# A two-block transformer kernel: x split for the second block without its inverse norm, three additions of eight on GpSimd, and weights, loads and chunks in another order

## The chip, the cores and the metric

The kernel runs on one core of a Trainium2 chip. The metric is the device time of one execution in microseconds, the median of several. All arithmetic is in fp32. The projections work with both operands split in two parts: a rounded high part and the rest, the low part, multiplied in three matmuls (high by high, high by low, low by high).

## The reference

The input x has 512 tokens of width 1024. It passes four mixers; the first two have no feed-forward block. `mem` has 256 rows that every token reads. Cut to what matters:

```python
def rms_norm(x, g):
    return x * rsqrt(mean(x * x, axis=-1) + EPS) * g

# first_block, i = 0, 1
hn = rms_norm(h, norm_pre[i])
proj = hn @ (w_in_a if i == 0 else w_in_b)   # i == 1: q, k, v, f_logit, q_m, gate
main = mla_mixer(...) if i == 0 else fox_mixer(q, k, v, f_logit, b_f)
mem_out = memory_attention(q_m, k_m, v_m)    # k_m, v_m = rms_norm(mem) @ w_mem_kv[i]
y = concat([main, mem_out]) * silu(gate)
h = h + rms_norm(y @ w_out[i], norm_post[i])

# second_block, layer = 0, 1
mod = silu(c) @ ada_w[layer] + ada_b[layer]  # shift, scale, gate, for mixer and for ffn
h = rms_norm(x, norm_mix_g[layer]) * (1 + sc_m) + sh_m
y = even_mixer(h) if layer == 0 else odd_mixer(h)    # HGRN2 and stick-breaking; mLSTM
x = x + g_m * y
h = rms_norm(x, norm_ffn_g[layer]) * (1 + sc_f) + sh_f
x = x + g_f * conv_glu_ffn(h)
# at the end: rms_norm(x, final_g)
```

The forget gate of `fox_mixer` is `log_sigmoid(f_logit + b_f)`, summed along the tokens. `odd_mixer` has a convolution over four tokens on q and k, and gates of its own.

## The kernel before

x is held transposed: eight tiles (`KT`) of 128 features by 512 tokens. A projection multiplies a weight chunk of 1024 by 256 (1 MB, eight pieces of 128 rows) with the eight tiles: 16 groups of three matmuls. `wide` makes the two outputs of a chunk together, piece by piece, so that it can start when the first tile of x is there. `features` makes one output, `tokens` the transposed form for values.

The five engines have programs written by hand, each in a fixed order, joined by semaphores. SyncE loads the chunks in the order of `weight_plan` into a ring of three places (`ring`); it waits until the place is free. Each chunk is split: ScalarE copies it to the rounded high part `wh` (`split_weights`, L1311), GpSimd subtracts that from the ring's copy and writes the low part `wl` (`low_weights`, L2240), which frees the ring's place. `wh` and `wl` have two places each (`SPLIT`), so ScalarE can split a chunk when TensorE has used up the one two before it. Between the projections' chunks stand 48 chunks of `ada_w`. VectorE multiplies each by silu(c) in eight operations (`ada_steps`, L1723 and L1725), which frees its place in the ring, and TensorE sums it over partitions (`ada_sums`, L524). `acc` has two places, so a step also waits for the sum of the one two before.

TensorE has six output banks in rotation (`bank`); a bank must be emptied by ScalarE or VectorE before it is opened again. `warm` (L475) is a matmul of the identity whose result nobody reads.

A norm goes like this: ScalarE squares a tile (`square`, L1336), TensorE sums over features (`ssq`, L557), VectorE makes the mean and its inverse (`inverse`, L1757 and L1759), ScalarE takes the root (`root`, L1350), TensorE spreads the row over partitions (`norm_spread`, L569), and VectorE multiplies. In `normed_split` VectorE writes the scaled tile (L1808), ScalarE rounds it to the high part (L1323; with a shift L1532), and VectorE subtracts for the low part (L1785; with a shift L1787). `xb` are the parts for the second block, `xe`, `xf` and `xo` those for the later ones.

`out_first(l)` is the output projection of block l = 0, 1. Behind it VectorE scales each tile of the result (L1946) and adds it to x (L1949), and the norm for the next block follows. Then the second block starts with `in_b.f` (one tile, the forget gates), `in_b.v` (three chunks in token form), `in_b.qm`, four chunks of `in_b.gate`, and three each of `in_b.q` and `in_b.k`. ScalarE empties their banks (silu for the gates). The forget gates' logarithm needs two table loads on ScalarE, a scan on VectorE, and 24 row DMAs from ScalarE's queue, which stand between the silus.

`out_second` is the output projection of the other stages; VectorE adds to x from the bank (L2110). The mLSTM block starts with `odd.gates`, then four chunks of `odd.qk`, four of `odd.v`, four of `odd.og`. VectorE convolves q and k (L2178, L2181) in eight steps and then does three ada steps. GpSimd stores the gates' maxima and loads them back, spread over partitions (`ho`).

## Time and profile before

| | us |
|---|---|
| median of 3 runs | 2054.84 |
| lowest, highest | 2053.12, 2055.91 |
| the profiled execution | 2056.67 |
| its span | 2054.9 |

The profiled execution's own time is 1.8 us more than its span. It is the one from which all durations come; times of events count from the start of its span. TensorE's granted clock was 0.99 of full over the whole, that is nearly always 2.4 GHz, else 1.2 GHz.

Busy times are 1976.8 us for TensorE, 1033.8 for VectorE, 778.6 for ScalarE and 784.3 for GpSimd. In TensorE's time are 84.0 us of the identity matmuls. The trace names the tile of `o1` "o". Some matmul records are missing, so counts in a stretch can be a little short.

### The profile page before, as it was taken

To read this page: it belongs to the slowest core of one execution; us is meant where nothing else is said; L and a number is where in the kernel's file an instruction comes from. 1 tells how busy PE (TensorE), PEld (TensorE's weight loads), DVE (VectorE), ACT (ScalarE), POOL (GpSimd) and SP (SyncE) were. 2 spreads that over 40 slices of the span, in tenths; PEclk is the share of its full clock that TensorE was granted. 3 is DMA by queue.
4 is the path that set the end of the run, shared out by engine and by line. 5 is a ranking of instruction groups with operands and counts; after the bars stand their busy time and mean duration, and the time that the engine had idled before them with its cause. 6 is when DMAs were issued, how large, how long until landed. Compare 5 with 4: busy or idle time off the path is not lost.

```text
span 2054.9 us, 23942 instructions
## 1 busy us (share of the span) xinstructions
PE 1976.8 (96%) x9958; PEld 1548.7 (75%) x9958; DVE 1033.8 (50%) x1508; ACT 778.6 (38%) x1192; POOL 784.3 (38%) x339
## 2 busy tenths in 40 slices
PE   7999998999999999999999999998899999999998
PEld 5875666688767598977788888776877777788776
DVE  5325566644576748734565646667711342311323
ACT  4333653423464432165432223323367332312331
POOL 2232553234463262212244344334433333344342
PEclk8999999999999999999999999999999999999999
DMA  7223104166402153111334444452421123233221
GB/s 238 79 57 81 54 1 133 57 189 188 143 1 82 62 166 101 62 62 41 103 124 159 153 138 136 130 171 70 157 82 42 62 82 103 67 98 122 75 75 57
DMA packets 203405, 205.73 MB, mean 100 GB/s; under 512 B 12023, under 2 KB 199675, under 8 KB 203296
## 3 DMA queue, kind: packets, MB, share of 16 engines
q1 hardware_dynamic: 200809, 200.31, 30.7%
q0 software_dynamic: 1472, 3.72, 0.7%
q8 instruction: 79, 1.29, 0.3%
q10 hardware_dynamic: 1015, 0.16, 0.0%
q14 instruction: 30, 0.25, 0.0%
HBM read 201.20 MB, written 2.11 MB: 99 GB/s over the span
## 4 chain that ended last, share of the span: by engine, by line
PE 74%; DVE 9%; POOL 7%; ACT 7%; issue 2%; DMA 1%; ACTq 0%; SPq 0%; DVEq 0%
PE bank L534 42%; PE bank L1102 15%; POOL wl L2240 6%; ACT wh L1311 3%; PE bank L768 3%; PE bank L475 2%; PE bank L792 1%; DVE conv L2131 1%; PE bank L925 1%; DVE conv L2133 1%; PE bank L817 1%; DVE conv L2129 1%; PE bank L1159 1%; PE bank L1169 1%; DVE acc L1725 1%
## 5 line engine op out<-in xcount | busy, mean ns | idle before, releaser
L2240 POOL TENSOR_TENSOR wl<-ring,wh 128x2048 fp32r<-128x2048 f32 (+3 forms) x146 | 634.9, 4349 | 984.1 <-ACT wh L1311 984.1
L1311 ACT ACTIVATE wh<-ring 128x2048 fp32r<-128x2048 f32 (+3 forms) x146 | 257.6, 1765 | 239.8 <-PE bank L1102 130.2
L1725 DVE SCALAR_TENSOR_TENSOR acc<-ring,cs,acc 128x256 f32<-128x256 f32 x336 | 288.9, 860 | 12.0
L534 PE MATMUL bank<-xfh,wh 128*128 128x512 f32 x704 | 277.3, 394 | 10.5 <-POOL wl L2240 8.1
L534 PE MATMUL bank<-xfl,wh 128*128 128x512 f32 x704 | 274.4, 390 | 0.0
L534 PE MATMUL bank<-xfh,wl 128*128 128x512 f32 x704 | 274.3, 390 | 0.0
L534 PEld LDWEIGHTS bank<-xfh,wh 128*128 128x128 f32 x704 | 132.2, 188 | 45.7 <-POOL wl L2240 16.7
L534 PEld LDWEIGHTS bank<-xfh,wl 128*128 128x128 f32 x704 | 132.2, 188 | 27.9
L534 PEld LDWEIGHTS bank<-xfl,wh 128*128 128x128 f32 x704 | 132.3, 188 | 26.4
L1102 PE MATMUL bank<-hsph,wh 128*128 128x512 f32 x352 | 138.3, 393 | 2.2 <-POOL wl L2240 2.2
L1102 PE MATMUL bank<-hsph,wl 128*128 128x512 f32 x352 | 137.2, 390 | 0.0
L1102 PE MATMUL bank<-hspl,wh 128*128 128x512 f32 x352 | 137.1, 389 | 0.0
L2110 DVE SCALAR_TENSOR_TENSOR x<-bank,mod,x 128x512 f32<-128x512 f32 x48 | 34.7, 751 | 192.8 <-PE bank L1102 192.8
L2262 POOL TENSOR_SCALAR probs<-probs,rinv 128x256 f32<-128x256 f32 (+2 forms) x96 | 100.2, 1056 | 59.5 <-DVE rinv L1919 59.5
L2129 DVE TENSOR_SCALAR conv<-a_raw,vecs 128x512 f32<-128x512 f32 x44 | 23.9, 544 | 196.6 <-ACT a_raw L1317 196.6
L1317 ACT ACTIVATE a_raw<-bank 128x512 f32<-128x512 f32 x44 | 26.4, 600 | 189.4 <-PE bank L534 187.6
L1723 DVE TENSOR_SCALAR acc<-ring,cs 128x256 f32<-128x256 f32 x48 | 37.5, 781 | 115.8 <-PE bank L524 100.0
L1336 ACT ACTIVATE sq<-x 128x512 f32<-128x512 f32 x56 | 35.2, 631 | 138.1 <-DVE x L2110 106.5
L1452 ACT ACTIVATE probs<-bank,nmx 128x256 f32<-128x256 f32 (+3 forms) x128 | 64.4, 511 | 54.2 <-DVE nmx L1916 53.6
L475 PE MATMUL bank<-consts 128*128 128x512 f32 x168 | 84.0, 627 | 0.0
L1102 PEld LDWEIGHTS bank<-hsph,wh 128*128 128x128 f32 x352 | 66.1, 188 | 16.9 <-POOL wl L2240 3.5
L1102 PEld LDWEIGHTS bank<-hsph,wl 128*128 128x128 f32 x352 | 66.1, 188 | 13.9
(397 smaller groups left out, 4151.8 us busy)
## 6 DMA issues: line engine op xcount, KB each, us to landing
ring<-in_ada_w SPq DMA_DIRECT2D x48, 1024.0 KB, 5.3
ring<-in_ffn_w_in SPq DMA_DIRECT2D x44, 1024.0 KB, 5.1
ring<-in_w_in_b SPq DMA_DIRECT2D x14, 1024.0 KB, 5.3
ring<-in_even_w_in SPq DMA_DIRECT2D x14, 1024.0 KB, 5.1
ring<-in_ffn_w_out SPq DMA_DIRECT2D x16, 768.0 KB, 4.5
ring<-in_odd_w_in SPq DMA_DIRECT2D x12, 1024.0 KB, 5.4
ring<-in_ffn_w_out SPq DMA_DIRECT2D x16, 640.0 KB, 4.1
ring<-in_w_out SPq DMA_DIRECT2D x8, 1024.0 KB, 4.9
```

The costliest lines, as they stand in the source:

```text
L475: eng.matmul(b[:, :], ident, consts[:, 0:S], start=True, stop=True)
L534: mm = eng.matmul(o, l_, r_, start=(first and i == 0), stop=(last and i == 2))
L768: eng.matmul(b[:, at_col:at_col + n], qf[0:kd, h, i * P:n], kf[0:kd, h, 0:n], start=first, stop=False, skip_group_check=True)
L1102: mm = eng.matmul(b[:, :], ws[a_][:, k, t * P:(t + 1) * P], xs[b_][:, k0 + k, :], start=(first and j == 0), stop=(end and j == 2))
L1311: eng.activation(wh[:, m % SPLIT, 0:w], ring[:, n % RING, 0:w], ACT.Copy).then_inc(wh_ready, 1)
L1336: eng.activation(sq[:, i % 2, :], src, ACT.Square).then_inc(sq_ready, 1)
L1452: ins = eng.activation(probs[:, par, po:po + n], b[:, c:c + n], ACT.Exp, bias=nmx[:, par, i:i + 1], scale=scale, accum_out=rsum[:, par, i: ...
L1723: chain.link(eng.tensor_scalar(s, w[:, 0, :], cs[:, 0:1], None, ALU.mult))
L1725: ins = eng.scalar_tensor_tensor(out=s, in0=w[:, k, :], scalar=cs[:, k:k + 1], in1=s, op0=ALU.mult, op1=ALU.add)
L2129: chain.link(eng.tensor_scalar(u, r[:, 0:S], vec(name, t), vec("ffn_conv_b_2", FT * l + t), ALU.mult, ALU.add))
L2240: eng.tensor_tensor(wl[:, m % SPLIT, 0:w], ring[:, n % RING, 0:w], wh[:, m % SPLIT, 0:w].bitcast(F32), ALU.subtract).then_inc(wl_ready, 1)
L2262: eng.tensor_scalar(w, w, rinv[:, par, i:i + 1], None, ALU.mult).then_inc(probs_ready, 1)
```

## The change

- **Second block.** x isn't normed before it is split. When a tile of x is complete, ScalarE writes its high part times the gain `norm_pre`, VectorE the low part. The projections' results are multiplied by the token's inverse norm: on VectorE for gates, f, qm, q and k, by rows copied to SBUF (`rows_rs`), on ScalarE for the values, by a column (`token_rs`). The first gate chunk is moved ahead of `in_b.f`, with the ssq matmuls between its pieces; silu becomes an operation of its own on ScalarE.
- **Additions.** Tiles 1, 3 and 5 are added to x by GpSimd (`residual`) at both borders. At the first GpSimd splits the chunk behind it afterwards, at the second it also waits for `mod_ready`.
- **Ada steps.** In the second block four stand behind the forget gates, and nine between the emptyings. In the mLSTM block one stands ahead of the convolutions, two between them. In the plan the ada chunks begin behind the first chunk of `in_b.v`, not the second.
- **mLSTM block.** The first chunk of `odd.qk` goes ahead of `odd.gates`; three identity matmuls are gone, and GpSimd splits up to the last `odd.v` chunk before it waits for the convolutions.
- **Half splits.** Behind `even_out` and `odd_out` the second chunk of the next stage is split in two halves.
- **Start.** The memory's squares all go ahead of the first weight split, VectorE's inverse ahead of the first low part; four half-width identity matmuls are added around the spread. At the border to the third block those between the ssqs are half as wide.

```diff
+SHARED = (1, 3, 5)
-    add(k8("in_b.f", w, 3 * MAIN, 3 * MAIN + P))
-    add(k8("in_b.v", w, 2 * MAIN, 3 * MAIN) + ... + k8("in_b.gate", w, 2572, 3596) + ...
-        + k8("in_b.k", w, MAIN, 2 * MAIN), (0,) + 13 * (1,))
+    gates = k8("in_b.gate", w, 2572, 3596)
+    add(gates[:1] + k8("in_b.f", w, 3 * MAIN, 3 * MAIN + P))
+    add(k8("in_b.v", w, 2 * MAIN, 3 * MAIN) + ... + gates[1:] + ... + k8("in_b.k", w, MAIN, 2 * MAIN), 13 * (1,))
...
@@ TensorE
-            def warm(count, aside=False):
+            def warm(count, aside=False, n=S):
...
+                if l == 0:
+                    return
                 for t in range(KT):
                     ssq(t, KT)
-                    warm(int(t < KT - 1))
+                    warm(int(t < KT - 1), n=S // 2)
...
+            m, ws = chunk("in_b.gate")
+            wide([("in_b.gate", t) for t in range(2)], "dve", ws, xb, KT, "x_b", behind=lambda k: ssq(k, KT))
+            chunk_done(m)
             m, ws = chunk("in_b.f")
-            features(("f",), "act", ws, slice(0, P), xb, KT, "x_b")
+            features(("f",), "dve", ws, slice(0, P), xb, KT, "x_b")
             chunk_done(m)
+            norm_spread("act")
+            b = bank(("token_rs",), "act")
...
+            project("odd.qk", 1, "act", "x_odd", xo)
             m, ws = chunk("odd.gates")
...
-            project("odd.qk", 4, "act", "x_odd", xo, fill=3)
+            project("odd.qk", 3, "act", "x_odd", xo, t=2)
...
@@ ScalarE
+            def split_half(m):
+                n = pe_at[m]
+                act.wait_ge(*released[m - SPLIT])
+                act.wait_ge(landed[n % RING], landing[n])
+                h = plan[n][2] * plan[n][3] // 2
+                eng.activation(wh[:, m % SPLIT, 0:h], ring[:, n % RING, 0:h], ACT.Copy).then_inc(wh_half, 1)
+                halved.append(m)
...
+                    if l == 0:
+                        eng.activation(xb[0][:, t, :], x[:, t, :], ACT.Copy, scale=vec("norm_pre", KT + t)
+                                       ).then_inc(xh_ready, 1)
                     square(x[:, t, :])
...
+            split_weights(tile_chunk[index[("in_b.gate", 0)]] + 3)
+            b = take(act, ("rs", 5), "act")
+            eng.activation(rows_rs, b[:, :], ACT.Copy).then_inc(emptied["act"], 1)
+            empty(("token_rs",), token_rs[:, :], part=(slice(0, P), slice(0, NB)))
+            def silu(t):
+                split_weights(tile_chunk[index[("in_b.gate", t)]] + 2)
+                wait_emptied(act, ("in_b.gate", t))
+                eng.activation(gate[:, t, :], gate[:, t, :], ACT.Silu).then_inc(silu_done, 1)
+            for t in range(2):
+                silu(t)
...
@@ VectorE
+                    if l == 0 and t >= 2:
+                        dve.wait_ge(xh_ready, used["x"])
+                        eng.scalar_tensor_tensor(out=xb[1][:, t - 2, :], in0=x[:, t - 2, :], scalar=vec("norm_pre", KT + t - 2),
+                                                 in1=xb[0][:, t - 2, :].bitcast(F32), op0=ALU.mult, op1=ALU.subtract
+                                                 ).then_inc(xl_ready, 1)
-                    if t >= 1:
+                    if 1 <= t <= KT and t - 1 not in SHARED:
...
-            normed_split([vec("norm_pre", KT + t) for t in range(KT)], tmp_b, xb)
+            inverse(KT, D)
+            def scaled_rows(key, dst, part=slice(0, P), scale=None):
+                b = tiles[index[key]][3][part, :]
+                if scale is None:
+                    return eng.tensor_tensor(dst, b, rows_rs[part, :], ALU.mult)
+                return eng.scalar_tensor_tensor(out=dst, in0=b, scalar=scale, in1=rows_rs[part, :], op0=ALU.mult, op1=ALU.mult)
...
@@ GpSimd
+            def residual(l):
+                for t in SHARED:
+                    pool.wait_ge(post_scaled, l * KT + t + 1)
+                    eng.tensor_tensor(x[:, t, :], x[:, t, :], o1[:, t, :], ALU.add).then_inc(x_shared, 1)
             attention(0)
+            low_weights(tile_chunk[index[("out_a", KT - 1)]] + 2)
+            residual(0)
             low_weights(tile_chunk[index[("out_a", KT - 1)]] + 3)
...
             attention(1)
+            low_weights(mark["att1"] + 5)
+            residual(1)
+            pool.wait_ge(mod_ready, 1)
             low_weights(mark["att1"] + 6)
...
-            low_weights(tile_chunk[index[("odd.v", 0, NB - 1)]] + 2)
+            low_weights(tile_chunk[index[("odd.v", 2, NB - 1)]] + 2)
```

VectorE at the border to the second block, before: the last additions, the norm of the new x, and its split.

```order
L1946 TENSOR_TENSOR o_85<-o_85,bank 128x512
L1949 TENSOR_TENSOR x<-x,o_85 128x512 x2
L1757 TENSOR_SCALAR var<-bank 128x128
L1759 RECIPROCAL var<-var 128x128
L1808 SCALAR_TENSOR_TENSOR tmp_b<-x,vecs,bank 128x512 x2
L1785 TENSOR_TENSOR xbl<-tmp_b,xbh 128x512
```

The same place in the changed kernel, from the first scaled tile on:

```order
L2002 TENSOR_TENSOR o_85<-o_85,bank 128x512 x2
L2011 TENSOR_TENSOR x<-x,o_85 128x512
L2002 TENSOR_TENSOR o_85<-o_85,bank 128x512
L2006 SCALAR_TENSOR_TENSOR xbl<-x,vecs,xbh 128x512
L2002 TENSOR_TENSOR o_85<-o_85,bank 128x512
L2006 SCALAR_TENSOR_TENSOR xbl<-x,vecs,xbh 128x512
L2011 TENSOR_TENSOR x<-x,o_85 128x512
```

The low halves `xbl` now stand between the scalings, ahead of the norm and not behind it; the additions of tiles 1, 3 and 5 are not in VectorE's row.

VectorE behind that, before: from the last low half through the forget gates' chain to the first ada step.

```order
L1785 TENSOR_TENSOR xbl<-tmp_b,xbh 128x512 x2
L1958 SCALAR_TENSOR_TENSOR frow<-frow 12x512
L1963 MEMSET frow 12x512
L1964 SCALAR_TENSOR_TENSOR frow<-frow 12x512
L1965 TENSOR_SCALAR frow<-frow 12x512
L1723 TENSOR_SCALAR acc<-ring,cs 128x256
```

And in the changed kernel:

```order
L1809 TENSOR_SCALAR var<-bank 128x128
L1811 RECIPROCAL var<-var 128x128
L2021 TENSOR_TENSOR gate<-bank,sq 128x512 x2
L2021 TENSOR_TENSOR frow<-bank,sq 12x512
L2037 SCALAR_TENSOR_TENSOR frow<-frow 12x512
L2042 MEMSET frow 12x512
L2043 SCALAR_TENSOR_TENSOR frow<-frow 12x512
L2044 TENSOR_SCALAR frow<-frow 12x512
L1775 TENSOR_SCALAR acc<-ring,cs 128x256
```

The inverse norm, two gate tiles and the product on the forget rows now stand ahead of the chain, and the ada step still behind it.

VectorE in the mLSTM block, before: from the gates' chain to the convolutions.

```order
L2168 SCALAR_TENSOR_TENSOR grow_140<-grow_137,grow_139 8x512
L2169 TENSOR_TENSOR grow_141<-grow_141,grow_140 8x512
L2178 TENSOR_SCALAR qkc<-qk_raw,vecs 128x512
L2181 SCALAR_TENSOR_TENSOR qkc<-qk_raw,vecs,qkc 128x512 x3
L2178 TENSOR_SCALAR qkc<-qk_raw,vecs 128x512
```

And in the changed kernel:

```order
L2262 SCALAR_TENSOR_TENSOR grow_139<-grow_136,grow_138 8x512
L2263 TENSOR_TENSOR grow_140<-grow_140,grow_139 8x512
L1775 TENSOR_SCALAR acc<-ring,cs 128x256
L1777 SCALAR_TENSOR_TENSOR acc<-ring,cs,acc 128x256 x7
L2273 TENSOR_SCALAR qkc<-qk_raw,vecs 128x512
```

One ada step has moved ahead of the eight convolutions.

## Rows read from the trace of the kernel before

**Rows 1.** The page: busy time, share of the span and instructions of each engine.

```profile
PE 1976.8 (96%) x9958; PEld 1548.7 (75%) x9958; DVE 1033.8 (50%) x1508; ACT 778.6 (38%) x1192; POOL 784.3 (38%) x339
```

**Rows 2.** TensorE's waits: who was waited for, us in total, times, longest.

```profile
PE bank L534 <- POOL wl L2240: 19.2, 23, 6.5
```

**Rows 3.** Timeline, VectorE, second block's border: start, us, instruction, count [idle before].

```profile
351.94 1.28 DVE L1946 TENSOR_TENSOR o<-o,bank 128x512 f32<-128x512 f32 x2 [1.98 <-PE bank L569]
353.14 2.59 DVE L1949 TENSOR_TENSOR x<-x,o 128x512 f32<-128x512 f32 x1
...
372.66 0.69 DVE L1785 TENSOR_TENSOR xbl<-tmp_b,xbh 128x512 fp32r<-128x512 f32 x1
374.05 0.68 DVE L1785 TENSOR_TENSOR xbl<-tmp_b,xbh 128x512 fp32r<-128x512 f32 x1
```

**Rows 4.** Timeline, TensorE: first matmuls of `in_b.v` and of two gate chunks.

```profile
383.30 0.28 PE L534 MATMUL bank<-wh,xbh 128*128 128x256 f32 x1
...
431.26 0.49 PE L534 MATMUL bank<-xbh,wh 128*128 128x512 f32 x1
...
442.64 0.49 PE L534 MATMUL bank<-xbh,wh 128*128 128x512 f32 x1
```

**Rows 5.** Timeline at the border to the third block, VectorE and TensorE.

```profile
682.69 2.52 DVE L1949 TENSOR_TENSOR x<-x,o 128x512 f32<-128x512 f32 x1
...
697.19 0.42 PE L557 MATMUL bank<-sq,consts 128*32 128x128 f32 x8
```

**Rows 6.** Timeline in the mLSTM block: TensorE, VectorE and SyncE's loads.

```profile
1402.29 2.74 PE L475 MATMUL bank<-consts 128*128 128x512 f32 x6
...
1417.26 0.50 PE L534 MATMUL bank<-xoh,wh 128*128 128x512 f32 x1 [1.33 <-POOL wl L2240]
...
1455.83 4.76 DVE L1723 TENSOR_SCALAR acc<-ring,cs 128x256 f32<-128x256 f32 x1
...
1464.27 0.37 SPq L1282 DMA_DIRECT2D ring<-in_odd_w_in  x1
...
1480.49 0.58 PE L534 MATMUL bank<-wh,xoh 128*128 128x256 f32 x1 [6.48 <-POOL wl L2240]
```

**Rows 7.** Timeline, GpSimd's subtractions beside rows 3: width 1024, then 2048.

```profile
338.72 2.55 POOL L2240 TENSOR_TENSOR wl<-ring,wh 128x1024 fp32r<-128x1024 f32 x1 [7.49 <-ACT wh L1311]
350.57 4.62 POOL L2240 TENSOR_TENSOR wl<-ring,wh 128x2048 fp32r<-128x2048 f32 x1 [9.30 <-ACT wh L1311]
```

**Rows 8.** GpSimd's groups by shape: busy us, mean ns, idle before.

```profile
L2330 POOL TENSOR_TENSOR og<-og,ho 128x512 f32<-128x512 f32 x8 | 10.3, 1285 | 15.3 <-ACT og L1317 15.3
```

**Rows 9.** Timeline in `in_b.v`: TensorE's wait, a load and its split.

```profile
395.97 0.39 PE L534 MATMUL bank<-wh,xbh 128*128 128x256 f32 x1 [1.00 <-POOL wl L2240]
...
404.41 0.37 SPq L1282 DMA_DIRECT2D ring<-in_w_in_b  x1
...
409.75 1.92 ACT L1311 ACTIVATE wh<-ring 128x2048 fp32r<-128x2048 f32 x1 [1.58 <-DMA ring<-in_w_in_b]
```

**Rows 10.** Timeline, two ada steps among q's chunks, and GpSimd behind the first.

```profile
489.06 7.90 DVE L1725 SCALAR_TENSOR_TENSOR acc<-ring,cs,acc 128x256 f32<-128x256 f32 x7
...
500.45 3.61 DVE L1725 SCALAR_TENSOR_TENSOR acc<-ring,cs,acc 128x256 f32<-128x256 f32 x7
...
504.33 4.67 POOL L2240 TENSOR_TENSOR wl<-ring,wh 128x2048 fp32r<-128x2048 f32 x1 [7.66 <-ACT wh L1311]
```

**Rows 11.** Stretches: length, busy times of the engines, granted clock, DMA share, GB/s.

```profile
16.60:26.50 9.90, 6.54 (x17) 5.14 (x18) 9.08 (x18) 5.05 (x11) 0.00 (x0) 0.50 1.08 363
...
373.50:383.20 9.70, 7.25 (x25) 4.01 (x25) 8.67 (x13) 3.78 (x6) 0.45 (x1) 1.00 0.01 2
...
1480.50:1484.10 3.60, 3.60 (x17) 3.60 (x18) 3.49 (x4) 1.06 (x1) 2.47 (x1) 0.50 0.69 198
```

**Rows 12.** GpSimd's subtraction behind the row DMAs in the gates' chunks.

```profile
460.95 4.66 POOL L2240 TENSOR_TENSOR wl<-ring,wh 128x2048 fp32r<-128x2048 f32 x1 [8.95 <-ACT wh L1311]
```

**Rows 13.** Timeline behind `even_out`: TensorE's wait for a low half of x.

```profile
1007.73 0.47 PE L534 MATMUL bank<-xfh,wh 128*128 128x512 f32 x1 [1.21 <-DVE xfl L1787]
```

177 lines of the change are left out of this document (114 added, 63 removed).

## The prediction, made before the changed kernel had run

> **What bounds the kernel now.** I read the page first: TensorE is busy 96% of the span [rows 1]. But that share counts the identity matmuls of line 475, which only keep the clock up. So what matters is where TensorE has no real work. The list of TensorE's waits gives the reasons, with low weight halves made by GpSimd first, 19.2 us [rows 2], and squares and low halves of x behind them. The gaps lie at a few borders. From the first scaled tile of the first block's output (351.94, [rows 3]) to the first matmul of `in_b.v` (383.30, [rows 4]), 31.4 us pass, in which TensorE does 24 useful matmuls at 0.23 us (5.4 us). In the stretch of `in_b.f` it follows VectorE's 1.4 us for each tile of x (372.66 to 374.05, [rows 3]). The border to the third block has the same form [rows 5]. In the mLSTM block one wait of 6.48 us stands between two chunks of `odd.v` [rows 6].
>
> One mechanism runs through all of it. A VectorE operation with both inputs in SBUF stops while GpSimd subtracts weights. The first `x<-x,o` took 2.59 us where this shape costs 0.68 unblocked (374.05), and ended after GpSimd's subtraction of 4.62 us [rows 3, 7]. One input in PSUM is enough to escape: `o<-o,bank` beside the same subtraction took its 0.6 us each [rows 3].
>
> **Part 1, border to the second block.** Removed from the path: inverse, root, spread and eight scalings ahead of the first projection. Added: ssq between the matmuls, one 4-column matmul, and products by the scales when banks are emptied. I walked the new order through engine by engine: VectorE scales a tile (0.60 from start to start, a PSUM input), adds five of eight tiles (0.68, both in SBUF), makes eight low halves (0.75, both in SBUF); GpSimd adds three tiles. GpSimd's 128x512 add isn't in the trace; its product of that shape takes 1.285 us [rows 8], which I take. The bounds are 0.68 (VectorE's) and 2.55 (a 128x1024 subtraction, [rows 7]). The first add is no longer blocked (-1.9), since the next subtraction now stands behind the three adds. The first low half ends at 355.8, and TensorE starts the gate chunk there; before, its first projection there began at 373.50. GpSimd then subtracts `in_b.f` (2.55) from about 363 and holds up VectorE once; the last low half ends at 370.5. TensorE ends the gate chunk at 371.9, `in_b.f` at 377.6, and the spread (1.15) at 378.8. `in_b.v` isn't ready then: ScalarE splits its weights behind the root (1.9, until 375.8) and GpSimd needs 4.66 more, so it starts at 380.5. By then a gate chunk of 11.2 is done, which stood behind 383.30 before (431.26 to 442.64 is one with its ada sums, [rows 4]). Gain: 383.3 + 11.2 - 380.5 = **14.0**. What hides the silus, the copies of the scales and the forget gate is ScalarE's idle time during `in_b.v`.
>
> Some of it comes back. The plan's ada chunks move one place ahead against the projections: the ring has three places, so the third chunk of `in_b.v` can only be loaded when the first ada chunk is used up. VectorE does that behind the forget gate's chain. Before, that chain ran during the first chunk of `in_b.v` and nobody waited for the load behind it, issued at 404.41 [rows 9]. Now ScalarE has two copies (0.6, 0.2), a table load (1.28), two silus (0.6 each) and a split (1.9) ahead of it, so its logarithm ends near 389.5, VectorE's chain at 392.8, the ada step (3.96 unblocked, [rows 10]) at 396.8, the load 5.35 later (404.41 to 409.75, [rows 9]) at 402.2, ScalarE's split at 404.1, GpSimd's at 408.8. The second chunk ends at 404.1: a new wait of **4.7**. After such a wait the clock falls: following the idle 6.48 us it was granted at half (1.2 GHz), to 1484.1 [rows 11]. A stretch of 3.4 us at half costs **1.7**. The old wait of **1.0** at 395.97 goes [rows 9]. Bounds for this place: 0 (the chain is early enough) and 11.
>
> **Part 2, gates, q and k.** ScalarE's silu now waits for VectorE's product (0.69), behind it stand its row DMAs and then the split for the next chunk, which GpSimd finished at 465.61 and TensorE began on at 465.66: no slack [rows 12]. Three chunks, 0.7 + 0.2 + 0.3: **1.2**. For q and k VectorE takes over four half tiles a chunk (3.0 us by 0.75 each) and starts the ada step 2.1 us later. Before it took 8.25 us where GpSimd's subtraction blocked it and 3.96 where not, in turn, and the chunk behind the blocked one was ready at 509.00 when it was wanted at 511.20 [rows 10]. 2.2 us of slack less 2.1: **0.5** in all; bounds 0 and 4.
>
> **Part 3, border to the third block.** Three adds go to GpSimd, its subtraction waits for `mod_ready`, the identity matmuls between the ssqs are halved. Queued behind that GpSimd wait is one weight chunk, wanted 11 us after the projections begin. Before: add blocked (2.52), then eight ssqs with full-width identity matmuls between them; last ssq at 697.19 [rows 5]. After: VectorE's 13 operations and three locks end at 689.9, and the last ssq begins at 691.0. Gain **6.3** (bounds 4.5 and 7).
> The profile shows that a GpSimd operation of this shape costs 1.285 against VectorE's 0.68, on a shared door. The Trainium skill's page "Perfetto Trace Analysis", section "Optimizing Scalar/DVE Operations", says that moving work between these two might not help, because they share a read port. With all eight adds left on VectorE I get 691.2 instead of 689.9; by that rule both borders lose some 1.3 us each and the kernel would come out 2.6 us later.
>
> **Part 4, halves of a split.** Behind `even_out` and `odd_out` GpSimd's subtraction blocked a low half of x, and TensorE waited 1.21 [rows 13]. Split into halves, GpSimd is done at +6.2 us after the last tile instead of at +7.9, ahead of that low half. The first half (1.08 at the rate of a 128x1024) delays the last square by 0.15. Gain 2 x 1.05 = **2.1**; bounds 0 and 2.6.
>
> **Part 5, mLSTM block.** The q/k chunk goes first, so VectorE's 1.4 us a tile lies beside six matmuls (1.36) and not three; `odd.gates` runs unpaced (5.4), the identity matmuls go (2.74, [rows 6]), and a 640-wide subtraction stands where a 2048-wide one blocked a low half. First matmul 1390.8 for 1392.07, the chunk done at 1401.6, gates at 1407.0, the next chunk's weights at 1408.3 instead of 1417.26. Gain **9.0**. The wait of 6.48 came from a load issued at 1464.27, when the first ada step, standing behind eight convolutions, was done [rows 6]. Now the step stands ahead of them and ends near 1428, so the load is issued near 1438, for a need at 1464. Gain 6.6, and the half clock behind it (1480.5 to 1484.1) **1.7**. What is late next: convolutions, near 1465, with 23 us to spare.
>
> **Part 6, start.** The reordering of squares, root and weight halves brings the first product of the memory about 0.5 ahead. TensorE was granted 0.50 from 16.6 to 26.5 [rows 11], following waits of 1.2 and 2.3; identity matmuls now fill part of them, but an idle 3.7 remains. I take **1.5**; bounds 0.2 and 3.2.
>
> **Sum.** 1.5 + (14.0 + 1.0 - 4.7 - 1.7) + (-1.2 - 0.5) + 6.3 + 2.1 + (9.0 + 6.6 + 1.7) = 34.1. The profiled execution took 2056.67 (span 2054.9 and 1.8 around it) and would take 2022.6; it lies 1.8 above the median of the runs, 2054.84, so the median goes to **2020.7**.
>
> **The rivals.**
> A: the ring wait in `in_b.v` doesn't arise. For it: VectorE's chain is short. Against: the walk leaves it 4.7 late. 6.4 us less, with the start at its best 1.7 less: 2013.
> B: that wait is larger or goes on into qm and gates, each with a half clock, or the mLSTM block's load is again late because GpSimd blocks the early ada step (4.76 for a 0.35 operation was seen, [rows 6]). Some 9 us less gain: 2030.
> C: slower. If the ada step in q, k and gates ends over 14 us after its chunk's start, each of 9 chunks waits 3 us and loses 1.7 to the clock, 42 us in all, more than the gain: 2063. It decides from about 2.2 us of lateness on, and needs 4 more per chunk to reach the other side. Against it: PSUM inputs aren't blocked [rows 3], and one chunk's VectorE work is 3.0 + 3.96 + 4.67 = 11.6 against a beat of 11.4.
> D: the change does not do what it says, the early gate chunk only moves the wait and the loads bound all: within 0.2%. Against it: DMA is mostly idle in these stretches (share 0.01 in the stretch of `in_b.f`, [rows 11]).
>
> **Numbers.** A difference of 0.2% (4 us) is about what a measurement of this kernel can tell from none. Forecast (2016 to 2025) 0.53, A (2010 to 2016) 0.15, B (2025 to 2034) 0.27, C 0.03, D 0.02. A and B, with their bounds, and the forecast make 0.95 faster; I leave some 0.1 of A's and B's outside the range, since each may go further than I walked. Range 2010 to 2034: the bounds of parts 1 and 6 downward, those of parts 1, 2 and 5 upward. Faster 0.95, same 0.02, slower 0.03.
>
> **What would show it.** Right: TensorE's first `xb` matmul near 356, first `in_b.v` matmul near 380.5; a wait on `wl` near 404 of 4 to 5 us with a granted clock of 0.5 behind it; no wait over 2 us in `odd.v`; VectorE's `xfl` first operations at 0.75; the first `xe` matmul 6 us nearer to the last `out_b` one. Wrong: VectorE's products from PSUM over 0.8 us beside GpSimd; waits on `wl` in every q or k chunk; GpSimd's adds over 1.4 us; half clock through the early gate chunk after which it ends behind 375.

## The result and the profile after

The changed kernel takes 2020.09 us (median of 4 runs, 2017.73 to 2023.00). The kernel before took 2055.38 beside it (4 runs). The ratio is 0.983, with an interval from 0.9811 to 0.9848: 35.3 us less, where 34.1 were forecast. The profiled execution is the slowest of the four: 2023.0, with a span of 2021.3.

The page of the changed kernel, busy time of each engine, beside [rows 1]:

```profile
PE 1959.0 (97%) x9938; PEld 1543.3 (76%) x9938; DVE 1031.0 (51%) x1529; ACT 766.9 (38%) x1171; POOL 784.7 (39%) x347
```

The sums of busy time hardly differ. What went are waits. So I measured both traces from mark to mark on TensorE's timeline, where a mark is the first matmul of a stage. "Half clock" is the time in which TensorE was granted 1.2 GHz. In the first row it is counted from the first matmul, in the others within the stretch. "Spread" is the eight matmuls that spread the inverse norm of the output projection; at the second border I count from the last of them, at the third from the first:

| stretch | before, us (half clock) | after, us (half clock) | gain | forecast |
|---|---|---|---|---|
| start of the span to first `out_a` matmul | 298.4 (20.5) | 295.4 (10.2) | 3.0 | 1.5 |
| from there to first `out_b` matmul | 329.6 (3.4) | 322.1 (10.2) | 7.5 | 6.9 |
| third border, spread to first `xe` matmul | 23.08 (3.4) | 19.83 (6.8) | 3.3 | 6.3 |
| the waits behind `even_out` and `odd_out` | 1.21 + 1.22 | none | 2.4 | 2.1 |
| mLSTM, start of the last sums of squares ahead of it (`sq_sum`) to the gates' turn (L1147, after: L1171) | 122.8 (6.8) | 106.3 (0) | 16.5 | 17.3 |
| all else | | | 1.0 | 0 |

The gains sum to the 33.7 us between the two spans. Of "all else" 1.3 us came at the very end, where the changed one had 2 us less of half clock. In the first row the load of `mem` let TensorE begin at 7.28 us before and at 8.62 after; from its first matmul on the gain is 4.4 us. In the third row the two have unequal clocks too, see below.

**Second border.** Timeline of the changed kernel, VectorE, then GpSimd, then TensorE: its first `xb` matmul, its last wait for a low half, the last sum of squares, the first matmul of `in_b.v`, and the one behind the ring wait:

```profile
353.25 1.76 DVE L2011 TENSOR_TENSOR x<-x,o 128x512 f32<-128x512 f32 x1
...
357.72 1.78 DVE L2011 TENSOR_TENSOR x<-x,o 128x512 f32<-128x512 f32 x1
...
360.30 2.01 DVE L2006 SCALAR_TENSOR_TENSOR xbl<-x,vecs,xbh 128x512 fp32r<-128x512 f32 x1 [0.20 <-ACT xbh L1517]
```

```profile
352.74 1.72 POOL L2369 TENSOR_TENSOR x<-x,o 128x512 f32<-128x512 f32 x1 [1.22 <-DVE o L2002]
357.22 1.73 POOL L2369 TENSOR_TENSOR x<-x,o 128x512 f32<-128x512 f32 x1 [2.76 <-DVE o L2002]
358.91 2.85 POOL L2341 TENSOR_TENSOR wl<-ring,wh 128x1024 fp32r<-128x1024 f32 x1
```

```profile
352.21 0.47 PE L540 MATMUL bank<-xbh,wh 128*128 128x512 f32 x1 [2.88 <-DVE xbl L2006]
...
362.36 0.50 PE L540 MATMUL bank<-xbh,wh 128*128 128x512 f32 x1 [0.84 <-DVE xbl L2006]
...
369.77 0.43 PE L563 MATMUL bank<-sq,consts 128*32 128x128 f32 x8
...
378.39 0.39 PE L540 MATMUL bank<-wh,xbh 128*128 128x256 f32 x1 [1.50 <-POOL wl L2341]
...
405.78 0.58 PE L540 MATMUL bank<-wh,xbh 128*128 128x256 f32 x1 [3.35 <-POOL wl L2341]
```

TensorE starts on the second block 4.0 us behind the spread (348.2), where it started 21.9 us behind it before (351.6 to 373.50), and then does a gate chunk and `in_b.f` beside VectorE's work. The low half that it waits for at 362.36 is the one of 2.01 us, held by GpSimd's subtraction. From there on it waits for nobody up to the end of the gate chunk at 370.1: it needs 1.94 us for a tile, six matmuls and a sum of squares. The price is the last row. It is the ring wait that was forecast: the load for the third chunk of `in_b.v` was issued at 393.97, when the first ada step behind the forget gates' chain was done (390.33 + 3.61 = 393.94).

```profile
389.96 0.34 DVE L1775 TENSOR_SCALAR acc<-ring,cs 128x256 f32<-128x256 f32 x1
390.33 3.61 DVE L1777 SCALAR_TENSOR_TENSOR acc<-ring,cs,acc 128x256 f32<-128x256 f32 x7
```

```profile
393.97 0.37 SPq L1306 DMA_DIRECT2D ring<-in_w_in_b  x1
```

**Granted clock.** Stretches of the changed kernel (length, busy times, granted clock, DMA share, GB/s): at the second border, behind the ring wait, and at the third border. TensorE was granted half in each, that is 1.2 GHz:

```profile
353.50:356.90 3.40, 3.40 (x16) 2.04 (x14) 3.21 (x4) 1.85 (x3) 0.96 (x1) 0.50 0.00 0
404.70:411.50 6.80, 5.72 (x27) 5.72 (x28) 6.58 (x7) 2.10 (x2) 3.97 (x2) 0.50 0.47 158
674.30:681.10 6.80, 6.80 (x42) 2.82 (x40) 4.75 (x10) 3.27 (x6) 5.01 (x3) 0.50 0.01 2
```

**Third border.** TensorE's timeline of the changed kernel. At half clock it takes 1.74 us from one sum of squares (L563) to the next, with an identity matmul (L481) between them, and it waits for nobody. At full clock it takes 0.98 (682.39 to 683.37), again without a wait:

```profile
673.51 0.43 PE L563 MATMUL bank<-sq,consts 128*32 128x128 f32 x8 [1.78 <-ACT sq L1370]
...
676.38 0.66 PE L563 MATMUL bank<-sq,consts 128*32 128x128 f32 x8
676.97 1.22 PE L481 MATMUL bank<-consts 128*128 128x256 f32 x2
678.12 0.65 PE L563 MATMUL bank<-sq,consts 128*32 128x128 f32 x8
...
682.39 0.43 PE L563 MATMUL bank<-sq,consts 128*32 128x128 f32 x8
...
683.37 0.43 PE L563 MATMUL bank<-sq,consts 128*32 128x128 f32 x8
```

**mLSTM block.** The first two chunks run without a stop from 1376.93 on. The wait of 6.48 us [rows 6] isn't there; the remaining one is the 1.15 of the third chunk. TensorE, then SyncE's load that in [rows 6] came at 1464.27:

```profile
1376.93 0.47 PE L540 MATMUL bank<-xoh,wh 128*128 128x512 f32 x1
...
1395.21 0.50 PE L540 MATMUL bank<-xoh,wh 128*128 128x512 f32 x1 [1.15 <-POOL wl L2341]
```

```profile
1425.14 0.58 SPq L1306 DMA_DIRECT2D ring<-in_odd_w_in  x1
```

### The profile page after: what moved, and what is told of

The parts are those of the page before. It is cut to its first block, busy times and chain, and to the rows that moved or that the text cites. A ratio compares the mean times of both kernels' runs of the same rounds, so it can differ in the third digit from the quotient of the medians.

```text
span 2021.3 us, 23916 instructions
## 1 busy us (share of the span) xinstructions
PE 1959.0 (97%) x9938; PEld 1543.3 (76%) x9938; DVE 1031.0 (51%) x1529; ACT 766.9 (38%) x1171; POOL 784.7 (39%) x347
## 4 chain that ended last, share of the span: by engine, by line
PE 76%; DVE 8%; POOL 7%; ACT 6%; issue 2%; DMA 1%; ACTq 0%; DVEq 0%; SPq 0%
PE bank L540 43%; PE bank L1125 16%; POOL wl L2341 6%; ACT wh L1336 3%; PE bank L781 2%; PE bank L481 2%; DVE conv L2225 1%; PE bank L805 1%; PE bank L948 1%; DVE conv L2227 1%; PE bank L830 1%; DVE conv L2223 1%; PE bank L1183 1%; PE bank L1193 1%; DVE acc L1777 1%
## 5 line engine op out<-in xcount | busy, mean ns | idle before, releaser
L2341 POOL TENSOR_TENSOR wl<-ring,wh 128x2048 fp32r<-128x2048 f32 (+4 forms) x146 | 620.0, 4247 | 962.0 <-ACT wh L1336 960.3
L1336 ACT ACTIVATE wh<-ring 128x2048 fp32r<-128x2048 f32 (+4 forms) x146 | 256.0, 1754 | 298.1 <-PE bank L1125 129.9
L1777 DVE SCALAR_TENSOR_TENSOR acc<-ring,cs,acc 128x256 f32<-128x256 f32 x336 | 281.3, 837 | 12.0
L2223 DVE TENSOR_SCALAR conv<-a_raw,vecs 128x512 f32<-128x512 f32 x44 | 23.9, 544 | 195.7 <-ACT a_raw L1351 195.7
L540 PE MATMUL bank<-xbh,wh 128*128 128x512 f32 x184 | 74.2, 403 | 4.1 <-DVE xbl L2006 3.7
L1125 PEld LDWEIGHTS bank<-hspl,wh 128*128 128x128 f32 x352 | 66.5, 189 | 13.6
```

The source lines that it names most:

```text
L540: mm = eng.matmul(o, l_, r_, start=(first and i == 0), stop=(last and i == 2))
L1125: mm = eng.matmul(b[:, :], ws[a_][:, k, t * P:(t + 1) * P], xs[b_][:, k0 + k, :], start=(first and j == 0), stop=(end and j == 2))
L1336: eng.activation(wh[:, m % SPLIT, h:w], ring[:, n % RING, h:w], ACT.Copy).then_inc(wh_ready, 1)
L1777: ins = eng.scalar_tensor_tensor(out=s, in0=w[:, k, :], scalar=cs[:, k:k + 1], in1=s, op0=ALU.mult, op1=ALU.add)
L2223: chain.link(eng.tensor_scalar(u, r[:, 0:S], vec(name, t), vec("ffn_conv_b_2", FT * l + t), ALU.mult, ALU.add))
L2341: eng.tensor_tensor(wl[:, m % SPLIT, h:w], ring[:, n % RING, h:w], wh[:, m % SPLIT, h:w].bitcast(F32), ALU.subtract).then_inc(wl_ready, 1)
```

## The experiments

All start from the changed kernel, whose median is 2020.1. Its own four runs lie 5.3 us apart, so medians tell only large differences. The stretches between marks in the profiles repeat to 0.1 us where the clock is the same, the longest (v to `out_b`) and the third border to 0.4. So each verdict rests on a stretch, and the median stands beside it. "v" is the first matmul of `in_b.v`; spread to v is 30.20 us in the changed kernel, and v to the first `out_b` matmul is 239.03.

### Does the gate chunk's place or the dropped norm carry the gain?

```diff
-    add(gates[:1] + k8("in_b.f", w, 3 * MAIN, 3 * MAIN + P))
+    add(k8("in_b.f", w, 3 * MAIN, 3 * MAIN + P) + gates[:1])
...
-            wide([("in_b.gate", t) for t in range(2)], "dve", ws, xb, KT, "x_b", behind=lambda k: ssq(k, KT))
...
+            wide([("f",)], "dve", ws, xb, KT, "x_b", behind=lambda k: ssq(k, KT))
...
+            wide([("in_b.gate", t) for t in range(2)], "dve", ws, xb, KT, "x_b")
```

(ScalarE's splits and VectorE's emptyings are put in the new order too)

> The changed kernel with the chunk of in_b.f ahead of the first gate chunk, as in the kernel before; all else (x split without its norm, ssqs between the pieces) stays. Theory: the gate chunk's second three matmuls per tile are what fills TensorE while VectorE makes the tiles; with f there it idles, and the gate chunk follows behind the last tile. From the spread of the first block's output to the first in_b.v matmul: 30.2 us in the changed kernel, 31.9 + 11.2 with a gate chunk's work added in the kernel before; here 33 to 35 (3.0 for the idle time, up to 2 more since GpSimd's 2048-wide subtraction of the gate chunk then falls into the split of x). 2024. Rival (the dropping of the norm alone carries the gain, VectorE's work sets the end in both orders): within 0.5 of 30.2, 2020.

Measured: 2027.19 (2023.24 to 2028.26), ratio 0.9864 [0.9849, 0.9879]; spread to v 35.89 us. That is 5.7 more, a little over the 3 to 5 that were expected. GpSimd's subtraction, VectorE's low half, and TensorE waiting for it:

```profile
358.99 4.97 POOL L2341 TENSOR_TENSOR wl<-ring,wh 128x2048 fp32r<-128x2048 f32 x1
```

```profile
360.37 4.13 DVE L2006 SCALAR_TENSOR_TENSOR xbl<-x,vecs,xbh 128x512 fp32r<-128x512 f32 x1 [0.20 <-ACT xbh L1517]
```

```profile
364.56 0.80 PE L540 MATMUL bank<-xbh,wh 128*128 128x512 f32 x1 [3.69 <-DVE xbl L2006]
```

The low half took 4.13 where it took 2.01 beside the 1024-wide subtraction. So of the 12.7 us that this border gained (31.67 + 11.2 - 30.20), 5.7 are the order of the two chunks. In this profile 13.7 us of the stretch were at half clock (3.4 in the changed kernel), which is part of the 5.7. The other 7.0 are what is left for the dropped norm, the shared additions (1.7, by the next experiment) and the first addition, which no longer meets a subtraction; no run has the norm alone.

### Do the shared additions pay?

```diff
-SHARED = (1, 3, 5)
+SHARED = ()
...
-                for t in SHARED:
+                for t in (1, 3, 5):
                     pool.wait_ge(post_scaled, l * KT + t + 1)
-                    eng.tensor_tensor(x[:, t, :], x[:, t, :], o1[:, t, :], ALU.add).then_inc(x_shared, 1)
```

> The changed kernel with all sixteen additions at the two borders on VectorE; GpSimd still waits for the same scaled tiles before its next subtraction, so that only the additions move. My walk: VectorE has three more operations of 0.68 at each border, 1.3 us later each: the first in_b.v matmul near 379.7 (378.4) and, at the third block, nothing, since TensorE sets that beat: 2021.4 in all, and up to 2022.7. The page's rule (the engines share a port, so moving work between them brings nothing or costs): the second border comes out 0 to 1.3 earlier, since GpSimd's additions, 1.65 to 1.76 each, held up two of VectorE's (1.76 and 1.78 in place of 0.68): 2019 to 2020.

Measured: 2019.91 (2017.27 to 2020.50), ratio 0.9829 [0.9814, 0.9844], no difference in the median. Spread to v is 31.88, that is 1.7 more. At the third border it is 18.34, as in the other profiles with as much half clock (3.4 us, 18.34 to 18.52): no difference. So the walk was right at the second border (1.3) and its account of the third held as well. The page "Perfetto Trace Analysis" of the Trainium skill, section "Optimizing Scalar/DVE Operations", says that such a move might not help since the engines share a port. The changed kernel's trace shows the two in each other's way: GpSimd's additions took 1.65 to 1.73 us where its product of [rows 8] took 1.285, and at the second border two of the three each held one of VectorE's for 1.1. The held ones began 0.5 us behind GpSimd's (353.25 and 352.74). Where VectorE's began first, by 0.2, it took its 0.68: once at this border, three times at the third. The move still paid 1.7 us where TensorE waits for VectorE's low halves, and nothing where TensorE sets the pace itself.

### The ring wait: three ways

First the plan: ada chunks begin behind the second chunk of `in_b.v`.

```diff
-        + k8("in_b.k", w, MAIN, 2 * MAIN), 13 * (1,))
+        + k8("in_b.k", w, MAIN, 2 * MAIN), (0, 1, 2) + 10 * (1,))
```

> The changed kernel with one edit in the plan: the first ada chunk of the second block stands behind the second chunk of in_b.v, as in the kernel before, and the next two behind the third chunk. The load of the third chunk then takes the ring's place of the first, which GpSimd frees near 378, not that of an ada chunk. Theory (ring): the wait on wl at 402.4 (3.35 us) and the half clock behind it (31 matmuls in 6.48 us where they take 3.8 at full clock) are both the plan's doing: both go, some 6 us, so 2014. Rival 1 (ScalarE is late, not the load): the wait stays at about 3 us, 2020. Rival 2 (the load that is now late is the one of qm or of a gate chunk): the wait moves one or two chunks on, 2018 to 2021.

Measured: 2018.27 (2015.67 to 2020.33), ratio 0.9823 [0.9808, 0.9838]; v to `out_b` 240.13. The wait in `in_b.v` is gone, and one of 4.44 stands at the second gate chunk, as the second rival had it. TensorE, SyncE's load for that chunk, and VectorE's step, which waits for TensorE's sum (L530) and frees the place:

```profile
430.78 0.79 PE L540 MATMUL bank<-xbh,wh 128*128 128x512 f32 x1 [4.44 <-POOL wl L2341]
```

```profile
418.65 0.37 SPq L1306 DMA_DIRECT2D ring<-in_w_in_b  x1
```

```profile
414.62 0.35 DVE L1775 TENSOR_SCALAR acc<-ring,cs 128x256 f32<-128x256 f32 x1 [7.95 <-PE bank L530]
```

Second the plan of the kernel before, with VectorE's new order kept.

```diff
-        + k8("in_b.k", w, MAIN, 2 * MAIN), 13 * (1,))
+        + k8("in_b.k", w, MAIN, 2 * MAIN), (0,) + 11 * (1,) + (2,))
```

> The changed kernel with the ada chunks of the second block where the kernel before has them: none behind the first chunk of in_b.v, one behind each later one, two behind the last. With the first three put later the wait had moved to the second gate chunk (4.44 us), as its load stood behind the third ada step, which waits for a sum. Here that load stands behind the second step (done near 407 there). Theory (the ring's order is all): neither wait, no half clock between in_b.v and the end of in_b.k, from the first in_b.v matmul to the first of out_b 239.0 less 3.4 less 2.7, so 233; 2014. Rival (VectorE is too late for any order, since the products stand among the steps): a wait of 2 us or more elsewhere in the block, 2018.

Measured: 2038.86 (2035.97 to 2039.74), ratio 0.992 [0.9903, 0.9936]; v to `out_b` 258.73, with 23.9 us of half clock. That is 19 us slower, and far beyond what I gave the rival. VectorE first, then ScalarE, then TensorE:

```profile
436.22 0.35 DVE L1775 TENSOR_SCALAR acc<-ring,cs 128x256 f32<-128x256 f32 x1 [1.97 <-PE bank L530]
436.61 3.61 DVE L1777 SCALAR_TENSOR_TENSOR acc<-ring,cs,acc 128x256 f32<-128x256 f32 x7
440.14 1.28 DVE L2021 TENSOR_TENSOR gate<-bank,sq 128x512 f32<-128x512 f32 x2
...
552.09 2.10 DVE L2022 SCALAR_TENSOR_TENSOR kf<-bank,sq 64x512 f32<-64x512 f32 x3
```

```profile
440.85 0.63 ACT L1540 ACTIVATE gate<-gate 128x512 f32<-128x512 f32 x1 [13.21 <-DVE gate L2021]
...
446.60 1.91 ACT L1336 ACTIVATE wh<-ring 128x2048 fp32r<-128x2048 f32 x1 [2.45 <-PE bank L540]
```

```profile
453.42 0.79 PE L540 MATMUL bank<-xbh,wh 128*128 128x512 f32 x1 [5.93 <-POOL wl L2341]
...
553.53 1.01 PE L781 MATMUL bank<-kf,qf 66*128 66x384 f32 x1 [5.74 <-DVE kf L2022]
```

Each ada step waits for a sum that TensorE now does one chunk later. Behind the step stand VectorE's products for the gates, behind a product ScalarE's silus and row DMAs (440.85 to 446.5), and behind these its split of the next chunk, at 446.60. TensorE wanted that chunk, the fourth of the gates, at 447.5. The load wasn't what was late: issued at 433.08, it landed at 438.59. A wait of 4.57 follows among q's chunks (484.20), and at the end the last products for k are late too, 5.74 us. The four waits over 0.5 us sum to 16.8, where the changed kernel has its one of 3.35; the rest of the 19.7 that v to `out_b` grew goes with 17 us more of half clock. This is the mechanism of rival C, and the theory that the ring's order is all has failed: an order on VectorE that has steps ahead of products can't bear a plan that is one chunk late. So the change's earlier ada chunks belong to its products, and the ring wait of 3.35 us came with them.

Third, the plan untouched, and one ada step ahead of the forget gates' chain, where VectorE was idle for 7.7 us.

```diff
+            ada_steps(1)
             wait_emptied(dve, ("f",))
...
-            ada_steps(4)
+            ada_steps(3)
```

> The changed kernel with one of the four ada steps ahead of the forget gates' chain on VectorE, where VectorE was idle for 7.7 us (379.3 to 387.0); the plan is untouched. Theory (the ring's place comes free late, since the step stands behind the chain): the step runs from 383.7 to 387.7, the third in_b.v chunk is loaded 6 us earlier (387.7 for 393.97), its low half is ready at 399.5 for a need at 402.1, the wait of 3.35 us and the half clock behind it are gone and nothing moves elsewhere, as the plan and so TensorE's sums are the same: from the first in_b.v matmul to the first of out_b 233 in place of 239.0, 2014. Rival 1 (it moves on, as with the two other plans): a wait of 3 us or more at qm or a gate chunk, 2018 or later. Rival 2 (the step is blocked by GpSimd's subtraction from 381.8 to 386.4 and ends near 391): about half of the wait goes, 2017.

Measured: 2013.69 (2011.92 to 2014.23), ratio 0.9796 [0.9783, 0.981]; v to `out_b` 232.92 with no half clock, where 233 was expected. VectorE, SyncE and TensorE:

```profile
379.44 0.33 DVE L1775 TENSOR_SCALAR acc<-ring,cs 128x256 f32<-128x256 f32 x1
379.81 7.85 DVE L1777 SCALAR_TENSOR_TENSOR acc<-ring,cs,acc 128x256 f32<-128x256 f32 x7
```

```profile
387.69 0.37 SPq L1306 DMA_DIRECT2D ring<-in_w_in_b  x1
```

```profile
402.48 0.36 PE L540 MATMUL bank<-wh,xbh 128*128 128x256 f32 x1
```

The load is issued at 387.69 as expected, but by another path: the step's data was there already, it began at 379.44, and took twice its time (7.85 for 3.61), beside GpSimd's subtraction from 382.02 to 386.86. TensorE finds its weights at 402.48. The whole cost of the ring wait was thus 239.03 - 232.92 = 6.1: 3.35 of waiting, and the other 2.8 with the half clock behind it. What was missing was a place for the step in VectorE's idle time, and not another plan.

### The third border and the clock

```diff
                 norm_spread((post_scaled, KT * (l + 1)))
-                warm(1)
+                warm(1 + 3 * l)
```

> The changed kernel with three more full-width identity matmuls behind the spread at the border to the third block, where TensorE idles for 1.78 us at 671.7. Theory (clock): the ssqs there follow each other at 1.72 us since TensorE runs at half clock from 674.3 to 681.2 and itself sets the beat; that clock fell because of the idle time. With it filled the clock stays up, the beat is VectorE's and ScalarE's (1.4, later 1.0), the last ssq begins near 680.5 in place of 683.4, and the kernel gains 2.5 to 3: 2017. Rival (the clock falls here whatever TensorE does, as it follows the last stages): the beat stays 1.7 and the kernel is 0 to 0.5 later, 2020.

Measured: 2017.62 (2015.62 to 2018.91), ratio 0.9817 [0.9801, 0.9834]; 17.59 us from the spread to the first `xe` matmul, no half clock; the changed kernel took 19.83 with 6.8 us of it.

```diff
-                    warm(int(t < KT - 1), n=S // 2)
```

> The changed kernel without the identity matmuls between the ssqs at the border to the third block. The same code there took 13.8, 12.3 and 11.0 us from the spread to the last ssq in profiles that had 6.8, 3.4 and 0 us of half clock in it. Theory: these matmuls are what the half clock stretches, since without them TensorE has 0.43 to 0.65 of work per tile where VectorE takes 1.4: 10.9 to 11.2 us whatever the clock, gain 0 to 2.8, 2018.5. Rival (they hold the clock up): half clock in this stretch for 6.8 us or more, and on into the first even chunk, where it costs 1.7 per 3.4: 2021 or later.

Measured: 2019.38 (2018.57 to 2020.09), ratio 0.9829 [0.9815, 0.9844]; 18.36 us, with 10.2 us of half clock, the most of all. TensorE of this kernel, where the last row is identity matmuls behind the sums, then the stretch:

```profile
674.22 1.32 PE L563 MATMUL bank<-sq,consts 128*32 128x128 f32 x16 [0.70 <-ACT sq L1369]
...
679.87 3.78 PE L481 MATMUL bank<-consts 128*128 128x512 f32 x4
```

```profile
674.00:684.20 10.20, 8.85 (x64) 3.67 (x65) 5.88 (x12) 4.26 (x8) 7.47 (x3) 0.50 0.01 2
```

The last sum of squares comes 10.2 us behind the spread at half clock, where it came at 11.0 at full clock with identity matmuls between (12.3 and 13.8 with 3.4 and 6.8 us of half clock). So those matmuls are what the half clock stretched, as the theory had it (with 10.9 to 11.2). But the low clock goes on into the next spread and the matmuls around it, as the rival had it, and takes the gain back. It is one profile, and the clock differs from one to the next, as the other kernels show. They have the same code at this border (the one with its additions on VectorE all but those):

| kernels | idle ahead of the first sum | half clock | spread to first `xe` matmul |
|---|---|---|---|
| changed; gates first | 1.78 | 6.8 | 19.83, 19.86 |
| forget first; whole splits; plan as before; ada behind conv; adds on VectorE | 1.78 | 3.4 | 18.35, 18.52, 18.49, 18.34, 18.34 |
| step ahead of chain; v chunks early; start as before | 1.78 | 0 | 17.02, 17.01, 17.01 |
| three more identity matmuls (two kernels) | filled | 0 | 17.59, 17.59 |

The same idle time is followed by none, 3.4 or 6.8 us of half clock, and each 3.4 cost 1.3 to 1.5 us. That the filled ones had none twice fits the theory, but three of ten unfilled ones had none either. Whether the identity matmuls prevent it stays open. If they do, they cost 0.6 (17.59 for 17.01) and still come out 0.7 ahead of the mean of these ten (18.3).

### mLSTM: the ada step, and the order of the chunks

```diff
-            ada_steps(1)
             dve.wait_ge(qk_pads, 1)
...
-                if t in (4, 7):
-                    ada_steps(1)
+            ada_steps(3)
```

> The changed kernel with the three ada steps of the mLSTM block behind the eight convolutions again. Theory: the wait of the fourth odd.v chunk for its low half comes back with 6 to 7 us, with half clock behind it (1.7): 2028. Rival (the order of odd.qk and odd.gates had already made the load early enough, or the half clock isn't tied to the wait): less than 3 us, 2020 to 2023.

Measured: 2026.75 (2026.58 to 2029.58), ratio 0.9868 [0.9853, 0.9883]. From the first `xo` matmul to the gates' turn it takes 108.85 us where the changed kernel takes 98.88: 10.0 more, of which a wait of 8.05, more than the 6 to 7 expected, and 1.9 with the half clock (10.2 us long, most of it on the wait itself). The chunk that waits is the third of `odd.v`, not the fourth. SyncE's load and TensorE:

```profile
1441.94 0.37 SPq L1306 DMA_DIRECT2D ring<-in_odd_w_in  x1
```

```profile
1453.82 0.58 PE L540 MATMUL bank<-wh,xoh 128*128 128x256 f32 x1 [8.05 <-POOL wl L2339]
```

```diff
-            project("odd.qk", 1, "act", "x_odd", xo)
             m, ws = chunk("odd.gates")
...
-            project("odd.qk", 3, "act", "x_odd", xo, t=2)
+            project("odd.qk", 4, "act", "x_odd", xo, fill=3)
```

(the plan and ScalarE's emptyings follow)

> The changed kernel with odd.gates ahead of odd.qk and three identity matmuls between them, as before; the ada step stays ahead of the convolutions. Theory (order of the two chunks): the last ssq of the feed-forward block to the end of the second chunk's matmuls grows by what the change saved there, 8.2 us (1371.1 to 1395.2 is 24.1, in the kernel before 32.3): 2028. Rival (the earlier ada step or the start of x's split gave part of it): 5 us or less, 2025.

Measured: 2028.40 (2027.33 to 2030.15), ratio 0.987 [0.9857, 0.9884]. First `xo` matmul to the gates' turn 105.71, 6.8 more, and ahead of it a wait of 1.13 (in the changed kernel none): 8.0, where 8.2 was expected. TensorE:

```profile
1376.19 0.43 PE L540 MATMUL bank<-xoh,wh 128*80 128x512 f32 x1 [1.13 <-DVE xol L1834]
...
1377.54 0.46 PE L540 MATMUL bank<-xoh,wh 128*80 128x512 f32 x1 [0.46 <-DVE xol L1834]
...
1401.33 0.50 PE L540 MATMUL bank<-xoh,wh 128*128 128x512 f32 x1 [1.26 <-POOL wl L2336]
```

The three identity matmuls come back in this kernel too (2.74 of [rows 6]); the two weren't taken apart.

### The halves, and the start

```diff
-            out_second("even_out", half=True)
+            out_second("even_out")
```

(and the same for `odd_out`)

> The changed kernel without the two splits in halves. Theory: the waits of 1.2 us for the low half of x behind even_out and odd_out come back, 1.1 and 1.3 us (so much the first xf matmul moved at each): 2.4 later in the trace, 2022.5. Rival (the other edits moved GpSimd's subtraction out of the way of the low half already): no wait, 2020.

Measured: 2022.47 (2020.62 to 2025.78), ratio 0.9846 [0.9831, 0.9861]; the first `xf` matmul 1.02 later at both (2.0 for the 2.4 expected), with the wait back:

```profile
991.43 0.47 PE L540 MATMUL bank<-xfh,wh 128*128 128x512 f32 x1 [1.14 <-DVE xfl L1839]
```

```diff
-            for k in range(4):
+            for k in range(2):
                 square_memory(k)
             split_memory(0, wh[:, 0, :])
-            root(2 * GROUP)
+            for k in range(2, 4):
+                square_memory(k)
             split_memory(1, wh[:, 1, :])
+            root(2 * GROUP)
...
-            inverse(4, D, 2)
             low_memory(0, wh[:, 0, :], wl[:, 0, :])
+            inverse(4, D, 2)
+            low_memory(1, wh[:, 1, :], wl[:, 1, :])
...
-            warm(2, n=S // 2)
             norm_spread((mem_normed, KT), 2)
-            warm(2, n=S // 2)
```

(and the transposes of the vectors ahead of the memory's sums again)

> The changed kernel with the start of the kernel before: two of the memory's squares behind the first weight split, the root behind the second, VectorE's first low part ahead of the inverse, no identity matmuls around the spread. From the first transpose (it waits for the load of mem, which lands at 7.3 to 8.6) to the first product of the memory the kernel before took 13.9 us and the changed one 13.2; from there to the first matmul of the first block 36.6 and 34.5. Theory: both come back, 2.8 us, of which some 2.1 is clock: 2023. Rival (the clock's part was chance, since the identity matmuls there don't hold it): 0.7 later, 2021.

Measured: 2018.82 (2017.83 to 2023.22), ratio 0.9826 [0.9812, 0.9839], so no loss in the median: both expectations missed it. From the first matmul of the kernel to the first of `out_a` it took 288.7 us. In the kernel before this was 291.1 with the same start, and in the twelve kernels with the new start 286.1 to 288.6, mean 287.5. By these the start is worth 1.3 to 3.7 us, on one profile each of the old start in the two kernels; the median doesn't show it, so what the new start gives stays open. One thing is regular there. At 102 to 112 us both kernels with the old start had 6.8 us of half clock, and all twelve with the new one 3.4.

### Three mends together

```diff
                 if l == 0:
+                    split_weights(tile_chunk[index[("in_b.gate", 0)]] + 3)
                 root()
```

with the step ahead of the chain and the filled third border, as above.

> As the one before, and two edits more: ScalarE splits the first in_b.v chunk ahead of the root (it waited for the gate chunk's end at 370.1 and then, behind the root, until 371.8), and at the third border three more identity matmuls fill the idle 1.78 us. Theory: the first in_b.v matmul 1.5 us earlier (28.7 from the spread, not 30.2), the third border at 11.6 us to the last ssq with no half clock in it: 6 + 1.5 + 0 to 2.2, 2011 to 2012.5. Rival (the root is then late and with it the spread, which must end ahead of in_b.v): 30 us from the spread, 2014.

Measured: 2009.43 (2008.07 to 2014.11), ratio 0.9781 [0.9765, 0.9797], faster than both kernels: 10.7 us under the changed one, and 1.6 under the expected range. Spread to v is 28.64, as expected, v to `out_b` 232.94, the third border 17.59. ScalarE splits ahead of the root, and TensorE goes from the spread into `in_b.v` without a wait:

```profile
368.88 1.92 ACT L1336 ACTIVATE wh<-ring 128x2048 fp32r<-128x2048 f32 x1 [2.33 <-PE bank L540]
370.70 0.29 ACT L1384 ACTIVATE var<-var 128x128 f32<-128x128 f32 x1
```

```profile
374.74 1.05 PE L575 MATMUL bank<-var,consts 128*128 128x128 f32 x8
375.63 0.28 PE L920 MATMUL bank<-consts,var 128*128 128x4 f32 x2
375.77 0.36 PE L540 MATMUL bank<-wh,xbh 128*128 128x256 f32 x1
```

## Why the prediction was right, point by point

The sum came out, 34.1 against 35.3 in the medians and 33.7 in the profiles. The experiments bear out the causes of the large terms, at the second border and in the mLSTM block. That the sum is so close is partly luck: the third border gave 3.0 less than forecast, and the start and "all else" 2.5 more, in both of which the clock had a part.

- **Part 1, the border: right, 1.3 too good.** Forecast 14.0, measured 12.7. The first matmul came 4.0 us behind the spread, as walked (4.2); the chunk ended 1.7 later than walked. Two terms were mis-sized. GpSimd's addition took 1.65 to 1.73 for 1.285, and two of them held VectorE's for 1.1 each, where I had one hold by the next subtraction. "GpSimd's adds over 1.4 us" was a sign of being wrong in my list; it came, and the additions on GpSimd still paid. And TensorE's own beat was missing: with the sum of squares it needs 1.94 a tile, and paced the last four tiles itself. The chunk ended 2.3 behind VectorE's last low half (367.86), and I had 1.4.
- **Part 1, ring wait: right in place and cause.** Forecast 4.7 near 404, measured 3.35 at 402.4 to 405.8. It is shorter because `in_b.v` began 1.3 later than walked and the weights were ready only 0.4 later (both against the spread), so these two errors are one and cancel. The half clock behind it was forecast at 1.7 and cost 2.8. Moving one ada step removed both, 6.1, where the forecast had 6.4.
- **Part 2: too dear.** Forecast 1.7 for gates, q and k. With the ring wait gone, v to `out_b` takes 232.9. Before it took 244.67, less the gate chunk of 11.2 and the old wait of 1.0: 232.5. The cost was some 0.4.
- **Part 3: half of it.** Forecast 6.3, measured 3.3. The failed step is that VectorE was taken for the bound and the clock for full. VectorE's 13 operations ended at 678.8, 7.9 us behind their start, but TensorE set the beat, with 1.74 a tile at half clock (0.98 at full). With no half clock the border takes 17.0, that is 6.1 us less than before. But the kernel before had 3.4 us of half clock there itself. At equal clock (18.34 to 18.52 with 3.4 us, for 23.08) the edits are worth 4.6 to 4.7. The three holds that I had counted on VectorE there didn't come: its additions took 0.68 each.
- **Part 4: right.** Forecast 2.1, measured 2.4; undone, 1.02 each.
- **Part 5: right.** Forecast 9.0 + 6.6 + 1.7, measured 16.5. Undoing the order gave 8.0, undoing the step 10.0.
- **Part 6: within its bounds** (0.2 to 3.2): 3.0 in the profile, but 4.4 from TensorE's first matmul on, above the bounds. Half clock there went from 20.5 to 10.2 us; undoing the edits brought back 1.3 of the 4.4, so the cause of the rest stays open.

Of the rivals, A (no ring wait) and D (nothing) didn't occur. B, a larger wait or one that goes on, didn't either: behind 405.8 TensorE has no wait over 0.5 us up to the first `out_b` matmul. C was argued away too lightly. The changed kernel stays clear of it, but with the ada chunks one place later it came, at 19 us. The reason I hadn't listed is the sums; the path, from a late product over the silus and row DMAs to the split, is the one without slack in part 2.

## What to carry to other kernels

A wait that a new order brings may stand for something that waits behind it, so look who holds the late buffer's place. Here a later chunk in the plan moved the wait or multiplied it, and one step put into an engine's idle time removed it. Where an engine holds both work that frees buffers and work that empties banks, its order and the loader's order are one decision. Work that needs no result yet (here a gate chunk on x without its norm) belongs beside the slowest producer.

## What the runs showed that I had not expected

- The same code with the same idle time of 1.78 us was followed by 0, 3.4 or 6.8 us of half clock. Each 3.4 cost 1.3 to 1.5 us where TensorE set the pace. The 5 us between executions of one kernel go with the clock: the changed kernel's four runs had mean clocks of 0.991, 0.991, 0.993 and 0.994 for 2023.0, 2021.9, 2018.3 and 2017.7 us.
- Where a wait for VectorE follows, half clock is nearly free. Spread to v took 30.20 with 3.4 us of it (353.5 to 356.9, ahead of the wait at 362.36), 30.22 with none and 30.53 with 6.8.
- A 128x512 addition on GpSimd took 1.65 to 1.74 us beside VectorE. It made VectorE's take 1.76 to 1.79 for 0.68, but only where GpSimd's had begun first.
- A late low weight half need not come from a late load. With the plan as before the load was there 8 us ahead of its split, and ScalarE's own order held it.
